# x turned as it lands, units awaited by quarters, picks over all rows, taps ahead of silus, z's end behind the convolution, pooling's evictions a step late

## The reference, cut to what matters

```python
# two hybrid layers (layers 0 and 1)
z  = rms_norm(x, norm_mix_w) @ w_in + b_in
aq, ak = rope(z[AQ]), rope(z[AK])                 # cos and sin of the positions
ya = dilated_mixture_attention(aq, ak, z[AV])
qk = silu(causal_short_conv(z[MQ:MV], conv_w, conv_b))     # four taps
hm = mlstm_chunkwise(mq, mk, z[MV], z[MI], z[MF])
yb = sigmoid(z[MO]) * rms_norm(hm) * mlstm_norm_w
x  = x + (sigmoid(z[GA]) * (ya @ w_proj_att) + sigmoid(z[GB]) * (yb @ w_proj_mlstm)) @ w_out
x  = x + square(relu(rms_norm(x) @ w_ff1)) @ w_ff2
# then a norm, and the layer with three branches (layer 2)
z, xbc, dt_raw, q, k, v, qi, ki, wi, u, gates = split(rms_norm(h, norm1_w) @ w_in)
xbc = silu(causal_dwconv(xbc, conv_w, conv_b))
dt  = softplus(dt_raw + dt_bias);  A = -exp(a_log)
y   = ssd_scan(xs, dt, A, Bm, Cm) + d_skip * xs   # needs prefix sums of dt * A
y_ssd  = rms_norm(y * silu(z), ssd_norm_w)
y_att  = attention over the 128 best keys of each query
y_pool = (mean over 2, 4, 8, 16 tokens - u) @ pool_w * pool_scale
h = h + (g0 * (y_ssd @ w_up_ssd) + g1 * (y_att @ w_up_attn) + g2 * (y_pool @ w_up_pool)) @ w_out
h = h + (silu(a) * b) @ w_ffn_out                 # a, b = split(rms_norm(h) @ w_ffn_in)
```

## Time and profile before

| | us |
|---|---|
| median of 3 executions | 2578.67 |
| lowest and highest | 2578.47 and 2582.0 |
| the profiled execution's own time | 2577.31 |
| its span, first to last instruction | 2575.5 |
| PE busy | 2481.9 (96%) |
| POOL, DVE, ACT busy | 1104.2, 986.6, 869.7 |

### The profile page before, as it was taken

One profiled execution on the slowest core, in us unless ns is written; L12 is line 12 of the kernel. 1 busy time (PEld: TensorE's weight loads), 2 busy tenths in 40 slices (PEclk: granted clock), 3 DMA queues, 4 the chain that ended last, 5 costly groups with the idle time before them and its releaser, 6 DMA issues. The chain is left out here.

```text
span 2575.5 us, 30104 instructions
## 1 busy us (share of the span) xinstructions
PE 2481.9 (96%) x11731; PEld 2005.3 (78%) x11731; DVE 986.6 (38%) x1578; ACT 869.7 (34%) x1089; POOL 1104.2 (43%) x808
## 2 busy tenths in 40 slices
PE   6999999999999999999999999989999799999998
PEld 5767688888888767788888887888776578888887
DVE  4455454310202445453311204646595444322201
ACT  4255333321324255333421324431325223322213
POOL 3432345454544432445454544432342245455543
PEclk9999999999999999999999999988999999999999
DMA  3311223322222311222322222221222122223221
GB/s 119 99 55 61 66 82 98 97 100 92 89 98 86 98 58 58 66 82 99 98 98 98 96 99 69 89 68 33 72 82 66 53 67 98 98 98 98 98 98 65
DMA packets 174011, 215.16 MB, mean 84 GB/s; under 512 B 7644, under 2 KB 155028, under 8 KB 173908
## 3 DMA queue, kind: packets, MB, share of 16 engines
q1 hardware_dynamic: 171236, 209.81, 25.3%
q10 hardware_dynamic: 2672, 3.89, 0.5%
HBM read 211.19 MB, written 2.10 MB: 83 GB/s over the span
## 5 line engine op out<-in xcount | busy, mean ns | idle before, releaser
L276 POOL TENSOR_TENSOR w_lo<-w_raw,w_hi 128x512 fp32r<-128x512 f32 x804 | 1104.0, 1404 | 1444.1 <-ACT w_hi L267 1444.1
L267 ACT ACTIVATE w_hi<-w_raw 128x2048 fp32r<-128x2048 f32 x201 | 385.0, 1915 | 1045.8 <-PE ps L308 393.3
L707 PE MATMUL ps<-h_hi,w_hi 128*128 128x512 f32 (+1 forms) x936 | 398.5, 426 | 1.9 <-DVE qk L2671 1.9
L707 PE MATMUL ps<-h_hi,w_lo 128*128 128x512 f32 (+1 forms) x936 | 371.0, 396 | 0.0
L707 PE MATMUL ps<-h_lo,w_hi 128*128 128x512 f32 (+1 forms) x936 | 370.1, 395 | 0.0
L306 PE MATMUL ps<-h_hi,w_hi 128*128 128x512 f32 x816 | 319.0, 391 | 0.0
L308 PE MATMUL ps<-h_hi,w_lo 128*128 128x512 f32 x816 | 317.5, 389 | 0.0
L307 PE MATMUL ps<-h_lo,w_hi 128*128 128x512 f32 x816 | 317.4, 389 | 0.0
L707 PEld LDWEIGHTS ps<-h_hi,w_hi 128*128 128x128 f32 (+1 forms) x936 | 176.6, 189 | 67.4 <-issue 29.8
L707 PEld LDWEIGHTS ps<-h_lo,w_hi 128*128 128x128 f32 (+1 forms) x936 | 176.8, 189 | 44.0 <-issue 8.4
L707 PEld LDWEIGHTS ps<-h_hi,w_lo 128*128 128x128 f32 (+1 forms) x936 | 176.1, 188 | 42.0
(11 more groups left out here) (399 smaller groups left out, 3676.3 us busy)
## 6 DMA issues: line engine op xcount, KB each, us to landing
w_raw<-in_w_in SPq DMA_DIRECT2D x72, 1024.0 KB, 5.2
w_raw<-in_w_ff SPq DMA_DIRECT2D x64, 1024.0 KB, 5.2
w_raw<-in_w_ffn_in SPq DMA_DIRECT2D x22, 1024.0 KB, 5.0
w_raw<-in_w_out SPq DMA_DIRECT2D x12, 1024.0 KB, 4.9
w_raw<-in_w_ffn_out SPq DMA_DIRECT2D x11, 1024.0 KB, 4.9
w_raw<-in_w_proj_att SPq DMA_DIRECT2D x4, 1024.0 KB, 5.0
w_raw<-in_w_proj_mlstm SPq DMA_DIRECT2D x4, 1024.0 KB, 5.0
w_raw<-in_w_up_ssd SPq DMA_DIRECT2D x4, 1024.0 KB, 5.2
```

The costliest lines, as they stand in the source:

```text
L267: act.activation(k.whi[:, slot * SLOT:(slot + 1) * SLOT], k.wraw[:, slot * SLOT:(slot + 1) * SLOT], ACT.Copy).then_inc(k.hi_done, 1)
L276: ins = pool.tensor_tensor(k.wlo[:, a:a + T], k.wraw[:, a:a + T], k.whi[:, a:a + T], ALU.subtract)
L707: mm = pe.matmul(out, lhs, rhs, start=i == 0 and n == 0, stop=stop and n == 2)
```

## The change

What it does, by place:

- **Quarters.** The lo chunks count one each on `split`, hi counts four. Unit 0 is rounded in four instructions (`hi_first`). In the lead, and in the first job of a unit that follows a unit of fewer columns than a slot has, PE waits for the quarter that it is about to read; elsewhere for all four as before.
- **Start.** `Params` no longer comes ahead of x on PE. The first norm's 8 columns are loaded and turned alone, into `first`. SP's order (`Loads`) is identity, first norm, unit 0, parameter rows, positions, table. The parameters are turned behind PE's piece 1, sums are hooked at 3, the spread at 7. `Angles` stands behind `Hand` on DVE; unit 1's hi stands behind the four pairs of x on ACT.
- **Rotary** is written out just ahead of rope, and rope waits for it.
- **First layers' conv and mLSTM.** Silus run four pairs behind the taps, evictions stand behind them. mLSTM joins the attention only, each head waits for its own silu, the spreads read all 128 rows of `gate_maxima`, zeroed ahead by DVE. The window is 18 for 16.
- **Layer 2.** The dt turn has 8 pieces, dt and decay 9, conv 36, SSD 54. The exponential of a_log moves into `Softplus`. xbc5 comes ahead of z2. The SSD picks read all 128 rows, zeroed ahead by DVE. The root's table is loaded ahead, and the last side evictions (hi among them) stand behind the root, `TAIL` is 8 for 4.
- **Pooling.** ACT and DVE emit side evictions up to share g, not g + 1.

```diff
-    def pick(self, h, n):
-
-        return self.cst[0:n, C_ID + h:C_ID + h + 1].broadcast_to([n, P])
+    def pick(self, h):
+
+        return self.cst[:, C_ID + h:C_ID + h + 1].broadcast_to([P, P])
...
-def wait_split(k, pe, u0, du=0):
-
-    pe.wait_ge(k.split, du + (u0 + 1))
+CHUNKS = SLOT // T
+
+
+def wait_split(k, pe, u0, du=0, part=CHUNKS):
+
+    pe.wait_ge(k.split, du * CHUNKS + (u0 * CHUNKS + part))
+
...
+def parts(i, cols):
+
+    return ((i + 1) * cols - 1) // T + 1
...
-        sp.wait_ge(k.split, du + (u0 - 1))
+        sp.wait_ge(k.split, du * CHUNKS + (u0 - 1) * CHUNKS)
...
-                   ACT.Copy).then_inc(k.hi_done, 1)
+                   ACT.Copy).then_inc(k.hi_done, CHUNKS)
...
+def hi_first(k, act):
+
+    act.wait_ge(k.landed[0], 16)
+    for a in range(0, SLOT, T):
+        act.activation(k.whi[:, a:a + T], k.wraw[:, a:a + T], ACT.Copy).then_inc(k.hi_done, 1)
...
+    def chunk(a):
+        pool.tensor_tensor(k.wlo[:, a:a + T], k.wraw[:, a:a + T], k.whi[:, a:a + T], ALU.subtract)\
+            .then_inc(k.split, 1)
...
         pool.wait_ge(k.hi_done, value)
         for a in range(slot * SLOT, (slot + 1) * SLOT, T):
-            ins = pool.tensor_tensor(k.wlo[:, a:a + T], k.wraw[:, a:a + T], k.whi[:, a:a + T], ALU.subtract)
-        ins.then_inc(k.split, 1)
-    with pool.Fori(0, n // 2) as i:
-        one(0, i * 2 + 1)
-        one(1, i * 2 + 2)
+            chunk(a)
+    for c in range(CHUNKS):
+        pool.wait_ge(k.hi_done, c + 1)
+        chunk(c * T)
+    one(1, 2 * CHUNKS)
+    with pool.Fori(1, n // 2) as i:
+        one(0, i * (2 * CHUNKS) + CHUNKS)
+        one(1, i * (2 * CHUNKS) + 2 * CHUNKS)
     if n % 2:
-        one(0, n)
+        one(0, n * CHUNKS)
...
+        if i == 0 or parts(i, cols) > parts(i - 1, cols):
+            wait_split(k, pe, u, part=parts(i, cols))
...
         lead = not self.units
+        short = not lead and self.words < SLOT
+        self.words = kt * cols
         self.units.append((u, src, cols))
...
+            job.last, job.lead, job.chunked = job is jobs[-1], lead, short and job is jobs[0]
             if job.n < 4:
...
+        if job.chunked and t in (None, t0) and i and parts(i, job.cols) > parts(i - 1, job.cols):
+            wait_split(k, pe, job.u, part=parts(i, job.cols))
         if i == 0 and t in (None, t0):
-            wait_split(k, pe, job.u)
+            wait_split(k, pe, job.u, part=parts(0, job.cols) if job.chunked else CHUNKS)
             if job.n >= 4:
...
         self.join(act)
-        for p in range(0, self.tiles + 2, 2):
-            self.come("act", act, p)
+        for p in range(0, self.tiles + self.ahead, 2):
+            if p < self.tiles:
+                self.side.emit_out("act", act, self.jobs[p + 1].end)
             for t in range(p, min(p + 2, self.tiles)):
-                if self.jobs:
-                    act.wait_ge(*self.ready(t))
+                act.wait_ge(*self.ready(t))
                 act.activation(self.dst[:, t * T:(t + 1) * T], self.tap(t, 0), ACT.Identity,
                                bias=k.col(self.bcol + t), scale=k.col(self.wcol + t))\
                    .then_inc(self.sem("tap"), 1)
-            for t in range(max(p - 2, 0), p):
-                act.wait_ge(*self.at("taps", t + 1))
-                d = self.dst[:, t * T:(t + 1) * T]
-                act.activation(d, d, ACT.Silu).then_inc(self.sem("silu"), 1)
+            p -= self.ahead
+            if p >= 0:
+                for t in range(p, p + 2):
+                    act.wait_ge(*self.at("taps", t + 1))
+                    d = self.dst[:, t * T:(t + 1) * T]
+                    act.activation(d, d, ACT.Silu).then_inc(self.sem("silu"), 1)
+                self.side_out("act", act, p, self.tiles)
     def dve(self, dve):
         k = self.k
         self.join(dve)
         for p in range(0, self.tiles, 2):
...
+        if self.also:
+            self.also(act).then_inc(self.sem("exp"), 1)
...
+        dve.memset(k.gm[:, :], 0.0).then_inc(self.sem("clear"), 1)
+        dve.wait_ge(*self.at("clear", 1))
...
-            pe.matmul(k.ps[:, 4 + h, :], k.pick(h, MH), k.gm[0:MH, :], start=True, stop=True)\
+            pe.matmul(k.ps[:, 4 + h, :], k.pick(h), k.gm[:, :], start=True, stop=True)\
               .then_inc(self.sem("spread"), 1)
...
+            pe.wait_ge(*self.conv.at("silu", MH + h + 1))
...
+        k, p = self.k, self.params
+        sp.dma_start(k.cst[:, 0:C_ROT], self.table[:, 0:C_ROT]).then_inc(self.sem("identity"), 16)
+        sp.dma_start(p.nrow[0:KD, :], p.norm).then_inc(self.sem("identity"), 16)
+        load_unit(k, sp, 0, 0, *self.units[0])
+        for prow, (rows, _) in zip(p.prow, p.sets):
+            for src, r, n in rows:
+                sp.dma_start(prow[r:r + n, :], src).then_inc(p.sem("landed"), 16)
+        self.angles.loads(sp)
+        sp.dma_start(k.cst[:, C_ROT:C_INV], self.table[:, C_ROT:C_INV]).then_inc(self.sem("table"), 16)
...
-        self.params.rows(act, slice(2, 3))
-        act.dma_start(k.cst[:, C_ROT:C_INV], self.table[:, C_ROT:C_INV]).then_inc(self.sem("table"), 16)
-        hi_unit(k, act, 0, 0)
-        self.join(act)
+        hi_first(k, act)
+        act.wait_ge(*self.params.at("cols", 1))
         for c in range(0, KD, 2):
-            if c == 4:
-                hi_unit(k, act, 1, 0)
             act.wait_ge(*self.at("turned", c + 1))
             act.activation(k.xT[:, c * T:(c + 1) * T], k.ps[:, c, :], ACT.Copy).then_inc(self.sem("fm_act"), 1)
             self.hand.hi(act, c)
             self.hand.hi(act, c + 1)
+        hi_unit(k, act, 1, 0)
         for t in range(KD):
             self.hand.square(act, t)
         self.hand.ahead = 2
     def dve(self, dve):
         k = self.k
-        self.join(dve)
+        dve.memset(k.eps[:, :], EPS)
+        self.params.norm_dve(dve)
         for c in range(1, KD, 2):
             dve.wait_ge(*self.at("turned", c + 1))
             dve.tensor_copy(k.xT[:, c * T:(c + 1) * T], k.ps[:, c, :]).then_inc(self.sem("fm_dve"), 1)
+        dve.wait_ge(*self.params.at("cols", 1))
         for t in range(4):
...
     def act(self, act):
-        k = self.k
-        self.join(act)
-        act.activation(self.s["A"], self.s["a_log"], ACT.Exp).then_inc(self.sem("exps"), 1)
         self.side_out("act", act, 6, self.STEPS)
-        act.wait_ge(*self.at("step", 9))
...
-        dve.wait_ge(*self.at("exps", 1))
+        dve.memset(self.rows[:, T:2 * T], 0.0).then_inc(self.sem("clear"), 1)
...
-    EACH, TAIL = 6, 4
+    EACH, TAIL = 6, 8
...
                 for h in range(g * SPG, (g + 1) * SPG):
-                    mm = pe.matmul(k.ps[:, 4 + h // 4, h % 4 * P:(h % 4 + 1) * P], k.pick(h, SH),
-                                   self.rows[0:SH, T + t * P:T + (t + 1) * P], start=True, stop=True)
+                    mm = pe.matmul(k.ps[:, 4 + h // 4, h % 4 * P:(h % 4 + 1) * P], k.pick(h),
+                                   self.rows[:, T + t * P:T + (t + 1) * P], start=True, stop=True)
...
+                act.activation(k.eps[:, 4:5], k.eps[:, 0:1], ACT.Sqrt)
             act.wait_ge(*self.at("gated", t + 1))
             act.activation(self.y[:, :], self.sz[:, t * D:(t + 1) * D], ACT.Square,
                            accum_out=k.stat[:, t:t + 1]).then_inc(self.sem("square"), 1)
-        self.side_out("act", act, self.EACH * TT, self.STEPS)
         act.wait_ge(*self.at("square", TT))
         act.activation(k.stat[:, 4:8], k.stat[:, 0:4], ACT.Sqrt, bias=k.eps[:, 0:1], scale=1.0 / D)\
            .then_inc(self.sem("root"), 1)
+        self.side_out("act", act, self.EACH * TT, self.STEPS)
...
-            self.side_out("act", act, g + 1, 5)
+            self.side_out("act", act, g, 5)
...
-            self.side_out("dve", dve, g + 1, 5)
+            self.side_out("dve", dve, g, 5)
...
-BESIDE1 = {"turn": 2, "forget": 5, "gates": 9, "rope": 14, "att": 40, "conv": 16, "mlstm": 54}
-BESIDE2 = {"turn": 4, "dt": 10, "decay": 10, "conv": 42, "ssd": 48, "select": 48, "att": 32, "pool": 24}
+BESIDE1 = {"turn": 2, "forget": 5, "gates": 9, "rope": 14, "att": 40, "conv": 18, "mlstm": 54}
+BESIDE2 = {"turn": 8, "dt": 9, "decay": 9, "conv": 36, "ssd": 54, "select": 48, "att": 32, "pool": 24}
...
+    loads = Loads(k, "loads", [], params, angles, table, [(weight(A["w_in"], 0, 0, D, AQ, UC), UC)])
+    setup = Setup(k, "setup", [], A["x"], params, loads)
+    params.free = setup.tile(KD - 1)
+    st += [loads, setup]
+    return setup, angles, params
...
-    st.append(hand)
+    st += [hand] if l else [params, hand]
...
+        qk_at = plain(AQ + j * UC, UC, [biased(qk[:, t * T:(t + 1) * T], t, B1 + t) for t in (2 * j, 2 * j + 1)])
+    side.hooks = {1: [params.turn], 3: [hand.sums], 7: [hand.spread]} if l == 0 else \
...
-    rest = add(Rest, "to_rope", side, max(at, qkv_at))
+    rest = add(Rest, "to_rope", side, max(at, qkv_at), qk_at)
     t1, t2 = k.at("rope_cos", o_scr, 2 * T), k.at("rope_sin", o_scr + 2 * T, 2 * T)
```

(51 more changed lines are left out.)

100 lines of the change are left out of this document (55 added, 45 removed).

## The result

| | median, us | range | ratio to before, 95% interval |
|---|---|---|---|
| before | 2579.29 | 2578.47 to 2582.0 | |
| changed | 2552.7 | 2549.34 to 2553.97 | 0.9893 (0.9876 to 0.991) |

The change is faster by 1.07% or 27 us, clear of the noise; 2522 was forecast, with 2506 to 2542. The sign is right and the size is not: half of the expected 56.5 came. The changed kernel's profiled execution has a span of 2551.8, 23.7 less.

A forecast was written before the change was run, and what follows sets the result against it. The prediction took TensorE to bound the kernel, busy 2481.9 of 2575.5 us, with standing and low clock to be won. Its terms summed to 56.5 us off the median 2578.67, giving 2522, range 2506 to 2542.

The forecast's parts named there:

- the rest of the 2482 us is fixed: Whole kernel: PE's order stays apart from one swap and no matmul goes, so only standing and low clock can be won.
- D: First layers' convolution and mLSTM: waits for last silus and low clock go, less new lo stalls; +7.9 us (4 to 12).
- A: Kernel start: w_0 lands sooner, the lead ends at 28.3 and job 4 starts at 46.0; +9.5 us (6 to 12).
- B: Unit behind the 8-column unit: PE waits by POOL quarters, so lo waits shrink; +3.3 us (2.5 to 3.3).
- C: Rotary, layer 0: sin, cos and their table load delay the rotary turn, a 6.8 stall; −6.5 us (−8 to −3).
- R2: Rival, chance 0.14: ACT's queue order holds back hi, cutting D by 3.5 and F to −2; 2531 us.
- F: Layer 2's convolution: last silu wait and low clock go, new waits of 2.3 and 0.9 come; +3.5 us (−2 to 8.7).
- E: Layer 2's dt region: waits for dt rows and lo go, less 0.4 for memset and DVE order; +6.2 us (4 to 6.6).
- G: SSD picks: reading 128 rows instead of 16 keeps PE's clock high; +8.5 us (0 to 11.9).
- H: SSD's tail: a 2.6 wait and 1.7 of clock go, a new 0.9 wait comes; +3.4 us (1 to 4.3).
- I: Pooling: evicting one step later removes four stalls and their low clock; +20.7 us (16 to 21.5).
- R3: Rival, chance 0.04: signalling each POOL quarter ends their overlap and slows the kernel, 2602 us at 1.1 per quarter.

The follow-up runs named there:

- arena_back: The changed kernel with its scratch arena starting 128 bytes further on, at 128 modulo 256 as before the change; 2529.13 us, ratio 0.9803.
- few_rows: The changed kernel with the SSD picks reading 16 rows and the mLSTM spreads 4 rows again; 2564.28 us, ratio 0.9941.

## Why the prediction was wrong, point by point

**What bounds, and "the rest of the 2482 us is fixed".** This sentence is the step that failed worst. It held the time of a matmul for fixed as long as the clock is: a term put at nothing, which measured 22.4. The change allocates one tile, `first`, and that moved the arena. Nothing in the profile of before shows it, but a comparison of the same line's mean over two operand tiles in the profile after does at once. Of the 34 us between the 56.5 forecast and the 22.9 of the table it is two thirds; nearly all the rest is D.

**A, start.** Right, mis-sized by 1.7. PE's timeline in the changed kernel:

```profile
4.88 0.27 PE L1820 MATMUL ps<-constants,all_params_norm 8*128 8x8 f32 x1 [4.88 <-DMA all_params_norm<-in_norm_mix_w]
5.08 5.81 PE L1925 MATMUL ps<-constants,setup_x 128*128 128x128 f32 x32
15.19 0.47 PE L347 MATMUL ps<-h_hi,w_hi 128*128 128x512 f32 x1 [4.30 <-ACT h_hi L387]
...
28.20 0.50 PE L735 MATMUL ps<-h_hi,w_hi 128*128 128x512 f32 x1
```

The lead ended at 28.20, where 28.3 was forecast, and job 4 began at 46.0, as forecast, 9.1 sooner than before. The rest of the gain came behind that: the kernel before has 3.4 us of low clock behind its stall of 1.92 there and the changed kernel none, worth 1.7 where 0.4 was put in. The stall before job 4 did not come in this trace (in arena_back it is 2.3); 1.5 stands at the sums instead.

**B** was as worked out, 1.9 in each layer. **C** was right in mechanism and place: a wait of 7.8 where 6.8 was forecast, and −6.1 for −6.5. The missing 1.0 is the mask, which took 0.55 in the kernel before with POOL idle and takes 1.57 here with POOL at work (102.14 to 107.24), for the 0.6 allowed. ACT and then DVE in the changed kernel:

```profile
102.08 1.28 ACT L2014 ACT_TABLE_LOAD   x1
103.37 0.63 ACT L2014 ACTIVATE sin<-setup_w 128x512 f32<-128x512 f32 x1
103.91 0.61 ACT L2015 ACTIVATE cos<-setup_w 128x512 f32<-128x512 f32 x1
```

```profile
104.55 1.57 DVE L2020 TENSOR_SCALAR cos<-cos,constants 128x512 f32<-128x512 f32 x1 [4.65 <-ACT cos L2015]
```

The table load takes 1.28 and sin starts 0.01 behind it. The drain that the Trainium skill, "ScalarE: Activation LUTs", section "What ACT_TABLE_LOAD costs", adds to a switch, 1.38 us, is not in these rows; the sum by the row was the better one.

**D** failed in its sum. What goes, 16.2, was right, and the first new wait of 3.5 is within the 2.2 to 4.2 given. But I counted one new wait and half a chance of low clock for each layer. There were two, 3.53 and 2.55, and 0.5 more on DVE, each of the two with 3.4 of low clock (1.7 of time): 2 × 10.0 came for 16.2 that went, or −3.8, where the matched starts say −3.0. The step "half a chance of a 1.7 clock loss" was optimistic, and the queue that an eviction moves past was read only up to the first unit. R2 (queue order eats D and F) had this mechanism, but took 3.5 off D where 10.9 went. F held: the two lo waits that it placed at 2.3 and 0.9 are 1.92 and 0.95. (Its lower end rests on a wrong sum: the wait of 6.4 and its 3.4 of clock are 9.8, not 10.7.)

**E and F** were 1.9 short in arena_back, where 3.4 of low clock stands in the dt region, and 0.5 short in the changed kernel's own trace, which has none there. Both have a wait of 2.2 that the earlier trace rows does not show, for the decay's first DVE step. PE is there at 1633.12, and DVE ends the eight passes of the first norm at 1634.15 and then does the new memset; I allowed 0.4 for all of it:

```profile
1628.80 5.35 DVE L550 SCALAR_TENSOR_TENSOR xT<-xT,all_param_cols,ps 128x512 f32<-128x512 f32 x8
1634.38 0.48 DVE L2067 MEMSET s_rows<- 128x512 f32 x1 [0.23 <-issue]
1634.78 0.36 DVE L2069 SCALAR_TENSOR_TENSOR s_small<-s_small,stat 128x64 f32<-128x64 f32 x1
```

**G** was right in its mechanism and too low: 8.5 forecast, 10.7 to 12.2 by few_rows; the full loss came back, not half of the second stretch's. **H** was wrong in its sign: +3.4 forecast, and the new end is slower than the old one in the same kernel by 4.3 (medians) to 5.5 (spans). Instead of 0.9 the new order has a wait of 3.6 and 6.8 of low clock. I costed what stands behind the root, and not what the six more pieces push into the next stage ahead of `ys_hi`. That G and H together come within 1.3 of their forecast is luck: the two errors cancel. **I** was right within 0.5.

**R3**, POOL's signals, is out: POOL's busy time went down, from 1104.2 to 1096.6, and the quarter's median is 1292 ns where it was 1291 (least, median and most in ns; before, then changed):

```profile
L276 POOL TENSOR_TENSOR w_lo<-w_raw,w_hi x804: 1255/1291/2555, 17.1 to 2547.2; 128x512 fp32r<-128x512 f32 x161
L289 POOL TENSOR_TENSOR w_lo<-w_raw,w_hi x804: 1254/1292/3338, 12.3 to 2523.7; 128x512 fp32r<-128x512 f32 x161
```

The range missed by 10.7 us, because its bounds held only the parts of the change that were meant. Without the address effect the same kernel takes 2529.13, inside the range, though D and H lie below their own lower ends.
